# A hybrid streaming encoder layer on one core: the output projection as seven pairs of block products, with finished rows parked in DRAM

## The reference, cut to what matters

```python
merged = None
for bi, yb in enumerate((pool_y, sb_y, ml_y)):
    gated = yb * jax.nn.silu(cols(OFF_Z + bi * BRANCH_W, BRANCH_W))
    term = jax.nn.sigmoid(cols(OFF_GATE + bi * D_MODEL, D_MODEL)) * jnp.einsum('btw,wd->btd', gated, w_branch[bi])
    merged = term if merged is None else merged + term
y = jnp.einsum('btd,de->bte', merged, w_out).astype(x.dtype)
x_out = x + rmsnorm(y, g_post)
```

## Time and profile before

| | us |
|---|---|
| median of 3 runs | 2259.88 |
| the profiled execution, its own time | 2259.75 |
| its span in the profile | 2257.7 |
| PE busy | 2236.8 (99%) |
| DVE busy | 1463.2 (65%) |
| ACT busy | 903.1 (40%) |
| POOL busy | 169.9 (8%) |

### The profile page before, as it was taken

The page is one execution under the profiler, slowest core; times in us unless marked ns, Lnnn a source line. Parts: engine busy times, 40 slices in busy tenths (PEclk is TensorE's granted clock), DMA queues, the critical chain, the costliest instruction groups (busy, mean ns, idle before and its releaser), DMA issues.

```text
span 2257.7 us, 39914 instructions
## 1 busy us (share of the span) xinstructions
PE 2236.8 (99%) x16400; PEld 2192.2 (97%) x16400; DVE 1463.2 (65%) x1692; ACT 903.1 (40%) x1225; POOL 169.9 (8%) x224
## 2 busy tenths in 40 slices
PE   8999999999999999999999999999999999999997
PEld 7999999999999999999999999999888999999997
DVE  7876767657666666777666666666777687653234
ACT  6333433434334344444444444444654334222221
POOL 0000000000100000111000000000112122000000
PEclk9999999999999999999999999999999999999999
DMA  6453443633544444444444444446766666744443
GB/s 179 114 142 103 115 140 87 172 98 111 132 116 124 121 119 124 116 125 123 118 126 115 125 119 121 126 114 198 235 209 209 202 188 196 189 116 120 122 103 102
DMA packets 418028, 311.29 MB, mean 138 GB/s; under 512 B 11389, under 2 KB 379141, under 8 KB 416336
## 3 DMA queue, kind: packets, MB, share of 16 engines
q1 hardware_dynamic: 398720, 247.24, 39.8%
q0 software_dynamic: 18912, 61.25, 7.8%
q10 hardware_dynamic: 240, 0.52, 0.1%
HBM read 250.07 MB, written 58.90 MB: 137 GB/s over the span
## 4 chain that ended last, share of the span: by engine, by line
PE 97%; DVE 1%; DMA 1%; issue 0%; ACT 0%; DVEq 0%; SPq 0%; ACTq 0%
PE pp L865 65%; PE pp L1091 13%; PE pp L1278 8%; PE M L883 2%; PE pp L875 1%; PE pp L1331 1%; PE M L1195 1%; PE M L1216 1%; PE M L1115 1%; PE M L1052 1%; PE M L875 1%; PE M L1255 1%; PE M L1144 1%; DMA gt_lo<-gated_scratch 0%; PE M L865 0%; PE M L983 0%
## 5 line engine op out<-in xcount | busy, mean ns | idle before, releaser
L865 PE MATMUL pp<-xa,wa_hi 128*128 128x288 f32 x7392 | 1480.4, 296 | 0.5 <-DVE wa_lo L1756 0.4
L865 PEld LDWEIGHTS pp<-xa,wa_hi 128*128 128x128 f32 x7392 | 1185.0, 188 | 1.8 <-issue 0.6
L865 PE MATMUL pp<-xa,wa_lo 128*128 128x288 f32 x3696 | 1086.6, 294 | 0.0
L865 PEld LDWEIGHTS pp<-xa,wa_lo 128*128 128x128 f32 x3696 | 696.2, 188 | 0.0
L1756 DVE TENSOR_TENSOR wa_lo<-raw_a,wa_hi 128x1024 fp32r<-128x1024 f32 x262 | 326.0, 1247 | 238.4 <-ACT wa_hi L1349 238.4
L1349 ACT ACTIVATE wa_hi<-raw_a 128x1024 fp32r<-128x1024 f32 x262 | 276.6, 1056 | 203.3 <-PE pp L865 202.3
L1756 DVE TENSOR_TENSOR wa_lo<-raw_r,wa_hi 128x1024 fp32r<-128x1024 f32 x134 | 170.6, 1273 | 140.1 <-ACT wa_hi L1349 140.1
L1349 ACT ACTIVATE wa_hi<-raw_r 128x1024 fp32r<-128x1024 f32 x134 | 141.4, 1055 | 133.2 <-PE pp L865 125.9
L1091 PE MATMUL pp<-gt_hi,wb_hi 128*128 128x288 f32 x768 | 168.9, 301 | 0.3 <-DMA gt_lo<-gated_scratch 0.3
L1091 PE MATMUL pp<-gt_hi,wb_lo 128*128 128x288 f32 x768 | 164.6, 296 | 0.0
L1091 PE MATMUL pp<-gt_lo,wb_hi 128*128 128x288 f32 x768 | 164.1, 295 | 0.0
(11 more groups left out here) (323 smaller groups left out, 2158.0 us busy)
## 6 DMA issues: line engine op xcount, KB each, us to landing
raw_a<-in_w_in_dram SPq DMA_DIRECT2D x202, 512.0 KB, 5.0
raw_r<-in_w_in_dram SPq DMA_DIRECT2D x68, 512.0 KB, 5.0
z_scratch<-zs POOLq DMA_DIRECT2D x60, 576.0 KB, 3.3
raw_b<-in_w_branch_dram SPq DMA_DIRECT2D x48, 512.0 KB, 5.0
raw_b<-in_w_out_dram SPq DMA_DIRECT2D x32, 512.0 KB, 4.8
gz<-z_scratch SPq DMA_DIRECT2D x48, 288.0 KB, 5.3
qkv<-z_scratch SPq DMA_DIRECT2D x22, 288.0 KB, 5.2
gt_hi<-gated_scratch SPq DMA_DIRECT2D x4, 1152.0 KB, 7.6
```

Of the source, the lines that this page charges most:

```text
L865: i = nc.tensor.matmul(out, ws[:, slot, k, :], xa[:, o, part, k, :], start=opens and k == 0 and s == 0, stop=k == HK - 1 and s == 2, skip_ ...
```

## The change

Tiles 0 to 13 of the output projection become seven pairs (`OUT_PAIRS`), each made with seven block products of 24 matmuls (`out_product`), A22 of a pair standing in the next pair or, for the last, alone (`OUT_LAST`). The operand blocks are `A11`, `A12`, `A22` of `merged` and four sums `S1` to `S4`. DVE forms the sums while the last branch runs (`form_sums`), for which that branch makes its tiles in the order 0, 8, 1, 9 ... 7, 15 (`tile_of`). S1 and S2 are split block by block; S3, S4 and the second token half of `merged` are split in the first pair, in instructions of 2304 columns (`late_hi`, `late_lo`, `second_half_hi`, `second_half_lo`).

The weights use the buffers and semaphores of the input projection's ring (`raw_a`, `wa_used`, ...) and `raw_o`; DVE forms four sums per pair. Results are put together from PSUM: ACT copies `os1`, `os5`, `os2` and the block Y21, DVE adds for Y11, Y12, Y22. Both tiles of a pair are turned together, in the third product of the next pair.

The operands now take the room of `y_tok` and `x_again`. So scaled rows of pairs 0 to 5 go to a small buffer (`stage`) and from there to DRAM (`y_scratch`, 0.66 MB each, on POOL's queue), and come back to `y_tok` near the end in two loads on SP's queue: 1280 columns (640 rows of 5,120 bytes, 3.28 MB) and 256 columns (0.66 MB). The gain is loaded in pieces, and all of `x_again` (rows of 8,192 bytes, 4.7 MB) is loaded after the sixth product of the last pair begins to free buffers. Tiles 14 and 15 keep their four parts, with own weight buffers `oc_hi`, `oc_lo`; their k-loop starts in the second half.

The core of the diff:

```diff
+OUT_PAIRS = Y_FULL // 2
+OUT_FIRST = 7 * PAIRS - 8
+OUT_LAST = 7 * OUT_PAIRS - 1
...
+    t = h % KD
+    return t // 2 + HK * (t % 2) if h >= H_ML else t
...
+        merged_lo = sb("merged_lo", R + 36864, [P, KD, T], F32R)
+        m_hi = sb("m_hi", R + 82944, [P, KD, T], F32R)
+        m_sums = sb("m_sums", R + 82944, [P, KD, T])
+        s12 = sb("s12", R + 119808, [P, 2, 2, HK, TH], F32R)
+        s12_sums = sb("s12_sums", R + 119808, [P, 2, 2, HK, TH])
+        s43 = sb("s43", R, [P, 2, 2, HK, TH], F32R)
...
+        stage = m_sums[:, 0:NB, TH:TH + 2 * P]
...
+        y_tok = sb("y_tok", R + 119808, [P, NB, D])
+        x_again = [sb(f"x_again{m}", R + at, [P, D]) for m, at in enumerate((0, 8192, 18432, 26624, 160768))]
...
+                if j < 2:
+                    sp.wait_ge(wa_lo_ready, made(out_at(OUT_PAIRS - 1, 1)))
+                else:
+                    sp.wait_ge(wb_lo_ready, H_OUT + j - 1)
+                d, k0 = (Y_FULL + j // 2) * P, 0 if j % 2 else HK
+                sp.dma_start(raw_b[:, j % 2, :, :], w_out_v[:, k0:k0 + HK, d:d + P]).then_inc(wb_loaded[j % 2], 16)
+
+            def reload(a, b):
+                sp.wait_ge(y_spilled, 16 * b)
+                sp.dma_start(y_tok[:, :, 2 * P * a:2 * P * b], y_spill[:, :, 2 * P * a:2 * P * b]).then_inc(y_reloaded, 16)
+
+            last_weights(0)
+            last_weights(1)
+            sp.wait_ge(wa_used, made(out_at(OUT_PAIRS - 1, 4)))
+            sp.wait_ge(t_ready, 4 * (PAIRS + OUT_PAIRS))
+            reload(0, OUT_PAIRS - 2)
+            last_weights(2)
+            last_weights(3)
+            reload(OUT_PAIRS - 2, OUT_PAIRS - 1)
...
+            def out_product(m, out, o, opens, ks=range(HK), hook=None):
+                pe.wait_ge(wa_lo_ready, made(m))
+                hi_, lo_ = form(o)
+                for k in ks:
+                    if k == HK // 2 and hook is not None:
+                        to_tokens(hook)
+                    for s, (ws, xs_) in enumerate(((oa_hi, hi_), (oa_hi, lo_), (oa_lo, hi_))):
+                        i = nc.tensor.matmul(out, ws[m % 3][:, k, :], xs_[:, k, :], start=opens and k == 0 and s == 0,
+                                             stop=k == HK - 1 and s == 2, skip_group_check=not opens and len(ks) == HK)
+                if ks[-1] == HK - 1:
+                    i.then_inc(wa_used, 1)
...
+                    out_product(out_at(0, 0), oa(0), A11, True, range(HK - 1))
+                    out_product(out_at(0, 2), od, A12, True, range(HK - 1))
+                    pe.wait_ge(mlo_ready, 2 * HK - 1)
+                    out_product(out_at(0, 0), oa(0), A11, False, [HK - 1])
+                    out_product(out_at(0, 2), od, A12, False, [HK - 1])
+                    pe.wait_ge(psum_read, H_OUT)
+                    pe.wait_ge(mlo_ready, 2 * HK)
+                else:
+                    if q > 1:
+                        pe.wait_ge(c21_done, PAIRS + q - 1)
+                    out_product(out_at(q, 0), oa(q), A11, True)
+                    pe.wait_ge(c22_done, PAIRS + q)
+                    if q == 1:
+                        pe.wait_ge(mlo_ready, A22_READY)
+                    out_product(out_at(q, 1), oa(q - 1), A22, False)
+                    pe.wait_ge(c11_done, PAIRS + q)
+                    out_product(out_at(q, 2), od, A12, True, hook=q - 1)
+                    pe.wait_ge(c12_done, PAIRS + q)
+                    if q == 1:
+                        pe.wait_ge(c21_done, PAIRS + 1)
+                out_product(out_at(q, 3), oc(q), S1, True)
+                pe.wait_ge(s1_ready, PAIRS + q + 1)
+                out_product(out_at(q, 4), oa(q), S2, False)
+                pe.wait_ge(s5_ready, PAIRS + q + 1)
+                if q == 0:
+                    pe.wait_ge(mlo_ready, S4_READY)
+                out_product(out_at(q, 5), oc(q), S4, False)
+                pe.wait_ge(s2_ready, PAIRS + q + 1)
+                if q == 0:
+                    pe.wait_ge(mlo_ready, S3_READY)
+                out_product(out_at(q, 6), oa(q), S3, False)
+            pe.wait_ge(c22_done, PAIRS + OUT_PAIRS)
+            out_product(OUT_LAST, oa(OUT_PAIRS - 1), A22, False)
...
+            def y21_out(q):
+                act.wait_ge(wa_used, made(out_at(q + 1, 1)))
+                act.wait_ge(ytr_done, 2 * q)
+                nc.scalar.activation(yT[:, 0, TH:T], oa(q), ACT.Copy).then_inc(c21_done, 1)
...
+            last_hi(0)
+            act.wait_ge(y_spilled, 16 * (OUT_PAIRS - 1))
+            second_half_hi(0)
+            last_hi(1)
+            last_hi(2)
+            y21_out(OUT_PAIRS - 1)
+            last_hi(3)
...
+                steps.link(nc.vector.tensor_tensor(x1, a21, a22, ALU.add))
+                steps.link(nc.vector.tensor_tensor(x2, x1, a11, ALU.subtract))
+                steps.end(1)
+                nc.vector.tensor_tensor(m_sums[:, k, TH:T], a11, a21, ALU.subtract)
+                nc.vector.tensor_tensor(m_sums[:, HK + k, TH:T], a12, x2, ALU.subtract).then_inc(xsum_ready, 1)
...
+            out_lo(out_at(0, 3), tx_o[:, :, :])
+            second_sum(0)
+            out_lo(out_at(0, 4), oraw_11(0))
+            late_lo(0)
+            out_lo(out_at(0, 5), oraw_22)
+            third_sum(0)
+            late_lo(1)
+            y11_out(0)
+            out_lo(out_at(0, 6), oraw_12)
+            dve.wait_ge(mlo_ready, S3_READY)
+            nc.vector.memset(stage[:, 2, :], 0.0)
+            fourth_sum(0)
+            second_half_lo(HK, 2 * HK + 3)
+            for q in range(1, OUT_PAIRS):
+                out_lo(out_at(q, 0), oraw_11(q))
+                y12_out(q - 1)
+                out_lo(out_at(q, 1), oraw_21(q - 1))
+                first_sum(q)
+                y22_out(q - 1)
+                out_lo(out_at(q, 2), oraw_21(q))
+                second_sum(q)
+                out_lo(out_at(q, 3), tx_o[:, :, :])
+                third_sum(q)
+                out_lo(out_at(q, 4), oraw_11(q))
+                fourth_sum(q)
+                y11_out(q)
+                scale_y(2 * q - 2)
+                out_lo(out_at(q, 5), oraw_22)
+                scale_y(2 * q - 1)
+                out_lo(out_at(q, 6), oraw_12)
...
+            last_lo(0)
+            second_half_lo(0, 2 * HK + 4)
+            last_lo(1)
+            last_lo(2)
+            last_lo(3)
+            scale_y(Y_FULL - 2)
+            scale_y(Y_FULL - 1)
...
+            def spill(q):
+                pool.wait_ge(yg_ready, 2 * (q + 1))
+                pool.dma_start(y_spill[:, :, 2 * P * q:2 * P * (q + 1)], stage).then_inc(y_spilled, 16)
...
-                pool.wait_ge(psum_read, H_OUT + 2 * (m + 1))
+                if m < 4:
+                    pool.wait_ge(wa_used, made(out_at(OUT_PAIRS - 1, 5 + m // 2)))
+                else:
+                    pool.wait_ge(wa_lo_ready, made(OUT_LAST))
                 prompt = min(rows, TP - at)
-                pool.dma_start(x_again[0:prompt, m, :], x_rows[at:at + prompt, :]).then_inc(x_again_loaded, 16)
-            pool.dma_start(x_again[prompt:rows, NT, :], x_sample[0, :, :]).then_inc(x_again_loaded, 16)
+                pool.dma_start(x_again[m][0:prompt, :], x_rows[at:at + prompt, :]).then_inc(x_again_loaded, 16)
```

## The result

| | median | of runs | range |
|---|---|---|---|
| before | 2260.05 us | 7 | 2259.75 to 2260.47 |
| after | 2266.3 us | 7 | 2263.61 to 2270.61 |

A forecast was written before the change was run, and what follows sets the result against it. PE was taken as the bound, 99% busy and without a gap in the chain. From 2259.75 us profiled, -22.4 + 4.1 + 0.7 + 9.1 + 2.0 = -6.5 gave 2253.25, as a median 2253.4; range 2244 to 2263.

The forecast's parts named there:

- Removed work: Output projection, seven tile pairs: 168 matmuls fewer at 0.1333 us each, 22.4 us saved.
- Steady pairs: Pairs 1 to 6: PE needs 23.5 us each and waits for neither DVE nor ACT, 0 us added.
- Rival 3: The pairs themselves make PE wait, 5 to 12 us on top of the forecast, 2258 to 2265; chance 0.13.
- First pair: First pair of the output projection: PE waits around the 2304-column splits, 4.1 us in sum.
- Last pair: Last pair: its lone A22 product waits until y22 has read the bank it adds onto, 0.7 us.
- End transfers: Tile 14: PE stops until tile 15's first weight block lands behind the parked rows, a wait of 9.1 us.
- Half to each queue: End part: 350 GB/s shared equally by SP's and POOL's queues, 175 each, tile 15's first block landing at T+9.2.
- T: The end of the last product; the prediction had x_again start to move at about T-5.
- After the stop nothing waits longer than before: End part: x_again's last bytes land at about T+20, the first finish comes at T+29 at the earliest.
- here the rows are long on both: End part: with rows of 5,120 and 8,192 bytes on the queues, 350 GB/s was assumed, going by the higher rates.
- rival 2: Load of tile 15's weights behind the parked rows: both queues together at 210 GB/s, wait 23 us, 2267.3; chance 0.12.
- Clock: Rest of tile 14's part after the stop: PE goes on at half clock, 2 us more.

The follow-up runs named there:

- e6: e2 with x_again loaded on SP's queue, behind tile 15's weights and the last parked rows: 2247.94 us, ratio 0.995.
- e1: The change, with POOL's loads of x_again waiting until tile 15's last weight block is in: 2249.98 us, ratio 0.9956.
- e4: The change, with each load of x_again cut in two, taking alternate 512-byte pieces, same bytes: 2252.37 us, ratio 0.9966.
- e3: The change with the edits of e1 and e2 together: 2248.36 us, ratio 0.9948.
- e7: e6, with the first pair's late splits behind the next weights and S3's low part ahead of Y11: 2246.16 us, ratio 0.9952.
- e8: e7, with the first finish waiting for x_again's first block and the parked rows alone: 2246.18 us, ratio 0.9937.
- e2: The change, with ACT's copy of Y21 ahead of the high part of tile 15's first block: 2267.62 us, ratio 1.0033.
- e5: The change, with POOL's last three gain loads one pair earlier, so x_again is asked for sooner: 2266.67 us, ratio 1.0029.

## Why the prediction was wrong

Its points in its own order:

- **Removed work, -22.4 us.** Right: 6 x 168 matmuls at 22.32 us each, 132.9 ns a matmul.
- **Steady pairs, 0.** Right, 23.41 against 23.5, with DVE and ACT near what was counted (16.9 and 11.7 a pair); from the second pair to the last product:

```profile
2056.60:2197.50 140.90, 140.74 (x1068) 140.50 (x1068) 97.77 (x147) 71.03 (x187) 8.61 (x12) 1.00 0.46 126
```

  that is 16.3 and 11.8 a pair. Rival 3 fell.
- **First pair, +4.1.** 2056.68 - 2033.13 = 23.55, less 19.2 of work: 4.35. **Last pair, +0.7:** 0.6. Right.
- **End transfers, +9.1.** Wrong in three ways. "Half to each queue" is not how the queues shared: they got one packet each, so that rows of 512 bytes beside 8,192 got a fourteenth of the bytes (0.11 against 1.55 MB). x_again was not under way at T-5 but asked for at T+1.4, as the gain loads in front of it took 5.5 to 6.5 us each, which made the first stop 4.3. And both weight blocks were treated as one that stands behind the parked rows, where the second one waits for raw_b behind a 2.5 us split and meets x_again in full.
- **The step that failed** is the sentence "After the stop nothing waits longer than before". It looked at x_again and its first user only and never asked when tile 15's second block lands. That block took 24.24 us, DVE's scaling stands behind its low part, ACT's squares behind that and PE's transposes behind those: 13.7 us. The prediction had a row with such weights and x_again both asked for, at 210 GB/s, and set it aside since "here the rows are long on both". They are long for the parked rows alone; the weights' are as short as in that row. Nor is the row itself, in the kernel before, a row of sharing in the main, as the prediction and its rival 2 took it. By queue, 2168 to 2170 has one entry:

```profile
q0 software_dynamic: 74, 0.48, 98.7%
```

  That is x_again alone, in two loads of 64 rows, at 238 GB/s; the weights start at about 2170.7, when it is nearly through.
- **Clock, +2.0.** Taken from the windows: after the first stop PE works at 0.50 from 2207.3 to 2212 and at 0.86 for 2 us, which loses 2.35 + 0.28; after the second at 0.50 from 2231.9 to 2236 and at 0.88 for 2 us: 2.05 + 0.24. Some 5 us, half of it per stop, where one stop was foreseen. The size per stop was about right.

Rival 2 had nearly the time (2267.3) and the sign, and in part the reason: low rate with both queues busy. That its time fits is luck: its place was wrong. It put the wait before the first block, which came in with the parked rows at 412 GB/s. And a low rate alone doesn't decide the sign: in e6 x_again runs at 193 for a while too, with no weights behind it, and the kernel is 0.5% faster than before.

With the second stop and its clock taken away (e1) the time is 2250.0, a gain of 10 where 6.5 was forecast, since the first stop was dearer in the forecast than it is. The arithmetic of the products was sound; the gain of 16.4 us at T was given back in the 23.7 behind it.

**A version that beats both.** e1 and e4 do by 0.4 and 0.3%, e3, e6, e7 and e8 by 0.5 to 0.6%; among the last four no order is shown. e7 is 2246.16 against 2260.05 before and 2266.3 for the change as given; e8 has the narrower runs and the same median.

## What to carry to other kernels

When a change shifts work in time, list every transfer that now falls into the same stretch, with its row length, and ask of the one with the shortest rows who waits for it; a small load with short rows beside a large one with long rows is the last to arrive, and one wait that holds the large one back can be worth as much as the change had gained before it (16.3 us here, of 16.4). A stop found in a forecast is not the last: take it out on paper and walk the same queues again, as e2 did on the chip, where removing the named stop gained nothing. Count packets by queue, and not only GB/s: two full queues can share in equal packets and very unequal bytes. And look at what starts a queue's big transfer, even small loads in front of it, since its moment decided here which stop was paid.

## What the runs showed of the hardware

- A load of 0.5 MB in 512-byte rows landed in 5.8 and 6.5 us with x_again held back (e1), in 24.2 and 25.8 beside 4.7 MB in 8,192-byte rows on another queue (after, e2), and in 8.1 beside those same bytes in packets of some 4 KB, asked for more slowly (e4).
- Two queues with work got packets one for one: 213 and 214 of 8,192 and mostly 512 bytes (after, 2208 to 2212), 95 and 97 of 8,192 and 5,120 (e5), 255 and 256 of 4,096 and mostly 1,024 (e4).
- The gain loads of 64 and 128 KB on POOL's queue took 5.5 to 6.5 us each (after), the first behind a parking of 0.66 MB on the same queue, all beside the parked rows on the other.
- Rows of 8,192 bytes on one queue, with as full engines, moved at 426 GB/s in loads of 128 rows and at 224 in loads of 64 (e1), at 238 in loads of 64 in the kernel before. In e6 it was 428 and then 193, from the first load of 64 rows into the next of 128. The cause was not varied.
- PE's granted clock was 0.50 (1.2 GHz) after stops of 4.3 and 13.7 us and for some 4.7 and 4 us of work behind them. After 2.3 us (e8) it fell too, and after 2.4 (e6) it stayed at 1.00.
